# Upper expert weights in halves of four rows a partition, in a mixture-of-experts step bound by its weight stream

## The reference, cut to what matters

```python
def clamped_swiglu(u):
    glu = jnp.minimum(u[..., :D_FF], SWIGLU_LIMIT)
    lin = jnp.clip(u[..., D_FF:], -SWIGLU_LIMIT, SWIGLU_LIMIT)
    return glu * jax.nn.sigmoid(SWIGLU_ALPHA * glu) * (lin + 1.0)
...
    def expert_chunk(args):
        xc, e = args
        return clamped_swiglu(xc @ w_up[e] + b_up[e]) @ w_down[e] + b_down[e]
```

## Time and profile before

| | us |
|---|---|
| median of 3 runs | 1422.34 |
| lowest and highest of them | 1421.0, 1423.39 |
| the profiled execution | 1423.31 |
| its span, first to last instruction | 1421.3 |
| expert stage, from the first upper matmul to the last sum | 482.7 to 1411 |

### The profile page before, as it was taken

One profiled execution on the slowest core, in us unless ns is written; L12 is line 12 of the kernel. 1 busy time (PEld: TensorE's weight loads), 2 busy tenths in 40 slices (PEclk: granted clock), 3 DMA queues, 4 the chain that ended last, 5 costly groups with the idle time before them and its releaser, 6 DMA issues.

```text
span 1421.3 us, 20600 instructions
## 1 busy us (share of the span) xinstructions
PE 1331.1 (94%) x8391; PEld 657.0 (46%) x8392; DVE 494.4 (35%) x1062; ACT 187.1 (13%) x403; POOL 101.7 (7%) x150
## 2 busy tenths in 40 slices
PE   6998879999899999999999999999999999999996
PEld 5887776777688533333333333333333333333332
DVE  2464646444541413223222232313222322233224
ACT  3221112323410200000000000000000000000001
POOL 1001123240000000000000000000000000000000
PEclk9999998999999999999999999999999999999998
DMA  6433339184679899999999999999999999999993
GB/s 187 136 106 83 73 64 289 62 303 130 220 249 358 339 423 430 430 429 431 431 431 431 430 431 431 431 431 430 430 432 431 431 431 431 431 431 431 432 431 145
DMA packets 87027, 479.94 MB, mean 338 GB/s; under 512 B 12740, under 2 KB 52918, under 8 KB 62008
## 3 DMA queue, kind: packets, MB, share of 16 engines
q1 hardware_dynamic: 78664, 452.00, 78.3%
q0 software_dynamic: 7600, 25.45, 5.0%
q10 hardware_dynamic: 704, 1.63, 0.3%
HBM read 478.60 MB, written 8.56 MB: 343 GB/s over the span
## 4 chain that ended last, share of the span: by engine, by line
PE 38%; DMA 26%; DVE 1%; issue 1%; ACT 0%; DVEq 0%; SPq 0%; POOL 0%; POOLq 0%; ACTq 0%
DMA ring<-in_w_up 25%; PE bank L2471 21%; PE bank L2492 9%; PE bank L2442 3%; PE bank L2485 1%; PE bank L2454 1%; PE bank L2424 1%; DVE x L2305 1%; DMA ex_work<-scratch_h,ex_si 1%; PE bank L2430 0%; PE bank L2052 0%; DVE ring L2393 0%; PE bank L238 0%; PE bank L2067 0%; DVE x L2402 0%
## 5 line engine op out<-in xcount | busy, mean ns | idle before, releaser
L2471 PE MATMUL bank<-ring,ex_work 128*64 128x512 f32 x2032 | 457.9, 601 | 18.6 <-DMA ring<-in_w_up 18.5
L2471 PEld LDWEIGHTS bank<-ring,ex_work 128*64 128x64 f32 x2032 | 141.4, 138 | 320.2 <-issue 286.5
L2492 PE MATMUL bank<-ring,ex_work 128*64 128x512 f32 x1024 | 235.2, 613 | 0.0
L2316 DVE TENSOR_SCALAR ex_work<-bank 128x512 f32<-128x512 f32 x32 | 22.1, 691 | 395.1 <-PE bank L2471 395.1
L2305 DVE TENSOR_TENSOR x<-bank,x 128x512 f32<-128x512 f32 (+1 forms) x192 | 117.2, 670 | 100.4 <-PE bank L2442 100.4
L2492 PEld LDWEIGHTS bank<-ring,ex_work 128*64 128x64 f32 x1024 | 72.6, 140 | 160.4 <-issue 160.4
L2442 PE MATMUL bank<-ex_work,ex_back 64*128 64x512 f32 x384 | 91.1, 606 | 1.5 <-ACT ex_work L2236 1.5
L578 PE MATMUL bank<-hT,w_group 128*128 128x264 f32 (+1 forms) x400 | 91.7, 391 | 0.0
L578 PEld LDWEIGHTS bank<-hT,w_group 128*128 128x128 f32 (+1 forms) x400 | 75.4, 189 | 15.2 <-issue 0.7
L2198 POOL DMA_INDIRECT ex_work<-scratch_h,ex_si x31 | 31.7, 1022 | 596.7 <-PE bank L2424 595.9
L2230 ACT ACTIVATE ex_work<-ex_work 128x512 f32<-128x512 f32 x32 | 20.1, 629 | 375.3 <-DVE ex_work L2316 375.3
(11 more groups left out here) (487 smaller groups left out, 1172.3 us busy)
## 6 DMA issues: line engine op xcount, KB each, us to landing
ring<-in_w_up SPq DMA_DIRECT2D x127, 2048.0 KB, 23.0
ring<-in_w_down SPq DMA_DIRECT2D x64, 2048.0 KB, 26.6
w_group<-in_w_in SPq DMA_DIRECT2D x12, 1024.0 KB, 5.3
w_cmp<-in_w_in SPq DMA_DIRECT2D x8, 1024.0 KB, 8.9
ring<-in_w_out SPq DMA_DIRECT2D x8, 512.0 KB, 7.0
out_win_s<-in_state_win_kv POOLq DMA_DIRECT2D x1, 4088.0 KB, 30.8
x<-in_x_prompt SPq DMA_DIRECT2D x4, 512.0 KB, 4.8
win_rows<-in_state_win_kv SPq DMA_DIRECT2D x4, 512.0 KB, 5.3
```

The source lines that it names most:

```text
L2471: mm = mmul(banks[n // 2][lo:lo + SLOTS, :], B["xT"][:, k % 4, SLOTS * (k // 4):SLOTS * (k // 4) + SLOTS], (ninth[:, k, :] if e_ninth and ...
L2492: mm = mmul(banks[4][SLOTS * n:SLOTS * n + SLOTS, :], B["hT"][:, k % 4, SLOTS * (k // 4):SLOTS * (k // 4) + SLOTS], slot_of(8 + 4 * half + ...
```

## The change

The upper matrix is laid out with four neighbouring rows on a partition. From expert 3 on it is moved in two halves of 512 rows (4 MB, runs of 32 KB) instead of four quarters. The first is issued when step 3 of the expert before is done, the second when all steps are; TensorE waits before steps 0 and 4 alone. `half_up` does this. Experts 0 to 2 and the second half of expert 31 move in quarters still: half of the columns of a home, runs of 16 KB at a distance of 32 KB (`upper_quarter`), with waits as before; the first half of expert 0 goes in one transfer. The step of the transposes becomes four, and `gain_columns` is turned to match. The ring has two upper homes of 4 MB and four lower of 2 MB, over the same memory; the transfers in the merge are put in another order, with a quarter of expert 0 ahead of expert 1's lower matrix.

```diff
-        pairs = [at(f"ring{i}", [P, 2, 2 * FF], z) for i, z in enumerate(
-            [DEAD, DEAD + PAIR, DEAD + 2 * PAIR, SEL + 4 * PAIR] + [SEL + PAIR * i for i in range(4)])]
+        upper = [at(f"ring_up{i}", [P, 4, 2 * FF], z) for i, z in enumerate((DEAD, SEL + 3 * PAIR))]
+        lower = [at(f"ring_down{i}", [P, 2, 2 * FF], z) for i, z in enumerate((SEL, SEL + PAIR, SEL + 2 * PAIR, DEAD + 2 * PAIR))]
...
+        def upper_half(e, i):
+            return a["w_up"][0][e, 512 * i:512 * i + 512, :].rearrange("(p c) n -> p c n", c=4)
+
+        def upper_quarter(sp, e, q):
+            cs = slice(2 * (q % 2), 2 * (q % 2) + 2)
+            sp.dma_start(upper[q // 2][:, cs, :], upper_half(e, q // 2)[:, cs, :]).then_inc(ring_in[2 * q], 16)
...
                     sp.wait_ge(outs.sem, 16 * 9)
-                    upper_weights(sp, 0, (0, 1))
+                    sp.dma_start(upper[0][:], upper_half(0, 0)).then_inc(ring_in[0], 16)
                     sp.wait_ge(mix_ok, KD)
                     bias_loads(sp)
-                    for e in range(2):
-                        lower_weights(sp, e)
+                    lower_weights(sp, 0, 0)
+                    lower_weights(sp, 0, 1)
+                    upper_quarter(sp, 0, 2)
+                    lower_weights(sp, 1, 0)
                     sp.wait_ge(od, KD)
-                    upper_weights(sp, 0, (2, 3))
+                    upper_quarter(sp, 0, 3)
+                    lower_weights(sp, 1, 1)
...
+                    def half_up(e, i):
+                        if i:
+                            sp.wait_ge(S["up_done"], e)
+                        else:
+                            sp.wait_ge(S["up_used"], 3 * (e - 1) + 2)
+                        sp.dma_start(upper[i][:], a["w_up"][0][bass.ds(e, 1), 512 * i:512 * i + 512, :].rearrange("e (p c) n -> (e p) c n", c=4)
+                                     ).then_inc(ring_in[4 * i], 16)
...
-                    up(1, True, (1, 2, 3))
-                    up(2, True, first_free=True)
+                    quarters(1, (1, 2, 3))
+                    quarters(2, range(4))
                     down(2, 0, True)
-                    up(3, True)
+                    up(3)
...
+                    half_up(NEXP - 1, 0)
+                    sp.wait_ge(S["up_used"], 3 * (NEXP - 1))
+                    upper_quarter(sp, NEXP - 1, 2)
+                    sp.wait_ge(S["up_done"], NEXP - 1)
+                    upper_quarter(sp, NEXP - 1, 3)
+                    down(NEXP - 1, 1, True)
...
-                            elif k == 0:
-                                pe.wait_ge(ring_in[k], 16 * e)
-                            elif k % 2 == 0:
-                                pe.wait_ge(ring_in[k], 16 * (e + 1))
+                            elif k == 0:
+                                pe.wait_ge(ring_in[0], 16 * e)
+                            elif k == 4:
+                                pe.wait_ge(ring_in[4], 16 * (e + 1))
```

More of the change, by code:

```diff
@@ L158, in build @@
         R["in"] = sem("route_consts_in", True)
-        R["gcol"] = sb(ctx, "gain_columns", [P, 4, 2])
+        R["gcol"] = sb(ctx, "gain_columns", [P, 2, 4])
         x = sb(ctx, "x", [P, 3, D])
@@ L2444, in comb, with up @@
                                 mm.then_inc(S["comb"], 1)
-                    def up(e, wait, back, late=False, first_pair=None, e_ninth=False):
+                    def up(e, wait, back, late=False, landed=None, e_ninth=False):
                         if late:
@@ L2462, in up @@
                                 turn_h(e - 1)
[L2463 to L2464 removed]
+                            if landed is not None and k % 2 == 0:
+                                if landed[k // 2] is not None:
+                                    pe.wait_ge(*landed[k // 2])
                             elif k == 0:
[L2466 to L2468 removed]
+                                pe.wait_ge(ring_in[0], 16 * e)
+                            elif k == 4:
+                                pe.wait_ge(ring_in[4], 16 * (e + 1))
                             for n in range(4):
```

59 lines of the change are left out of this document (28 added, 31 removed).

## The result

The changed kernel takes 1426.3 us (median of 20 runs, 1419.3 to 1430.0), the kernel before 1422.2 (20 runs, 1418.2 to 1426.8). The ratio, which goes by the means of the runs (1425.4 and 1422.5), is 1.0021, with a 95% interval of 1.0012 to 1.0031: some 3.0 us slower. The medians lie 4.1 us apart. A second series gave 1.0019 (1.0003 to 1.0034).

What follows compares the result with a forecast made beforehand. The prediction took the landing of expert 30's last upper quarter, set by the DMA stream, plus TensorE's remaining work as the bound; -2.2 + 3.4 + 1.5 = +2.7 us on the 1422.3 median gave 1425.0 us, range 1421.5 to 1430.

Steps and rivals of the forecast that it cites:

- within or slower: Cases for the whole time against the kernel before, about 0.2% being no change: within 0.46, slower 0.47, faster 0.07.
- term 3: Later issue of upper halves: the queue runs short at experts 3 and 17; +1.5 us, bounds 0 and 3.
- What bounds the end: End of the kernel: landing of expert 30's last upper quarter, set by the DMA stream, plus TensorE's remaining 61.6 us.
- Term 1: Upper-matrix stream: fewer, larger packets save a cost per packet, 0.0092 us a MB over 239 MB; -2.2 us, bounds 0 and 3.1 saved.
- Term 2: Tail at expert 30: four steps instead of two remain after the last upper landing; +3.4 us, bounds 1.7 and 5.1.
- 65 us from there to the end: Sign for the tail: time from expert 30's last wait to the end, 65 us instead of 61.6.
- Edits at nothing: Fewer issues, transposes' step, gather beside larger packets (7.2 us could double, covered), merge order, fewer semaphore waits: no cost.
- R1: Rival, faster: packets cost more and the tail is covered; upper stream over 1.2% faster, -4.2 us, 1418; chance 0.05.
- R2: Rival, slower: reads 32 KB apart are slower, 5.5 us of stream per cent lost; 1433 at 1%; chance 0.12.
- R3: Rival, slower: upper packets stay at 16 KB, so no saving; +4.9 us, 1427; chance 0.11.
- some 7300: Sign for the rate: the number of packets by which the changed kernel's count would fall.
- R4: Rival: saving and later issues cancel and the tail is hidden by TensorE getting ahead; -0.7 us, 1422; chance 0.10.

Runs made afterwards that it cites:

- wait_halves: Kernel before, with only TensorE's wait made coarser: a whole half of an upper matrix before steps 0 and 4; transfers, packets and issues unchanged; ratio 1.0014.
- wait_whole: Kernel before, with TensorE waiting for the whole upper matrix (all four quarters) before step 0, for all experts; ratio 1.0324.
- quarters_apart: Kernel before with the new row layout alone: quarters in 16 KB runs 32 KB apart, transposes at a step of four; ratio 1.0002.

## Why the prediction was right, and where its terms were not

The forecast of 1425.0 us, the range, and "within or slower" hold: 1426.3 us, and a ratio that lies at the bound of 0.2% between the two likeliest cases. Three mechanisms were named and all three act. That the sum comes out so near is partly luck: term 3 was priced at a third of its size, and what makes up for it is in part an effect that the prediction does not have.

- **What bounds the end.** Right. The last link through a transfer ends at 1359.2, where the second half of expert 30 lands, and the rest is TensorE's. (The flat stretch of the earlier trace rows is slices 15 to 38, from 533 to 1386 us, so some 850 us and not 890; nothing hangs on it.)
- **Term 1, predicted -2.2.** Right in mechanism and in size. Its 0.0092 us a MB, from the 421 GB/s beside the 431 of the earlier trace rows, is 4.8 ns a packet; measured are 4.7 from 16 KB to 32 KB and 4.7 from 8 KB to 16 KB. With the 0.01 for fewer transfers after gains 0.084 to 0.090 us an expert, over 28.5 experts 2.4 to 2.6 us. Two windows of a few microseconds gave this number; that another two (417 instead of 421) give 3.1 shows how much of the accuracy is chance. By the last landings the gain looks like 3.3 us, but there the shares' drifting apart in before is counted with it.
- **Term 2, predicted +3.4.** Right: +3.6 in `wait_halves` at the same clock, 32 matmuls behind the last wait. In after's profile it shows as 1.7, since the clock did not fall. The "65 us from there to the end" was met at the clock of before, and missed as it was profiled (63.4).
- **Term 3, predicted +1.5.** The mechanism and both places are right; the term was mis-sized: +3.65 by the last landings (1.34 at expert 3, 2.31 at 16 and 17), +4.4 by the mean of the signals (1.7 and 2.7), past its upper bound of 3 either way. The step that failed is to count from the last landing ahead, with a start-up of 2.5 us behind it. For the last share that step is right: in after the half of expert 17 went out 1.0 us ahead of the last landing (952.7 and 953.7), by the step 1.5 are lost, and the half landed 11.14 us behind the transfer ahead, where two transfers of 4.84 would be 9.68. But the other shares had landed from 949.8 on, so their engines lost more; that shows in the 2.4 us of missing bytes, and at the landings behind (10.49 and 6.11 us behind the one ahead for the second half of expert 17 and its last lower transfer, instead of 9.68 and 4.84). In `wait_whole` even 2.8 us ahead were not enough.
- **A term that is missing.** The sixteen shares lie closer together behind a gap. In before the last share lands 2.9 us behind the mean at T, in after 1.8. That takes 1.1 us off.
- **Edits at nothing.** Right: the distance of 32 KB and the step of the transposes by `quarters_apart` (1.0002). The gather got longer, not doubled: GpSimd waits 278.2 us over 30 for it, 9.3 each instead of 7.2, and TensorE nowhere waits for it.

```profile
POOL ex_si L2217 <- DMA ex_work<-scratch_h,ex_si: 278.2, 30, 11.2
```

- **The rivals.** R1 needed a stream over 1.2% faster in the upper halves: 0.09 us of some 19.5 an expert is 0.5%. The ceiling of 435.2 GB/s that the Trainium skill gives ("DMA: Bandwidth & Descriptors", section "Where 436 GB/s comes from") fits the 432 of after over 200 us; single slices of the profile of after, with 436 and 437, lie a little above it. R2 is excluded by `quarters_apart`. The loss at large row pitches that the Trainium skill gives ("DMA: Bandwidth & Descriptors", section "Latency and other measured facts": 207 GB/s of 214 at 512 KiB) does not show at a pitch of 32 KB here: 1.0002. R3 is excluded by 7424 packets of 32 KB, and 8607 packets fewer on the page, where some 7300 were announced; 1183 of them are packets under 512 B (12740 before, 11557 after). R4 needed a hidden tail, and `wait_halves` shows it in full.

The prediction's own sum would be, with the measured terms and the missing one, -2.5 + 3.6 + 4.4 - 1.1 = +4.4. The profiles have +2.6 with the clock's 1.7 us in after's favour, +4.3 without it. The timed difference is +3.0 by the means (interval +1.7 to +4.4), +4.1 by the medians. Since the clock falls in some executions and not in others, at one place or another, part of the difference between 4.4 and 3.0 stays open.

## What to carry to other kernels

Where a stream of transfers sets the time, a larger transfer has three prices: who reads it waits for all of it, its home is free only when all of it is read, and its issue comes that much later. The first is paid once, behind the last landing, and again wherever the reader's lateness delays an issue into a short queue. The others are paid wherever the queue is short. There one should ask for the time between the issue and the landings of the transfer ahead, and not the last of them alone. Over the upper transfers of the fourteen traces (from 505 us on), one issued 1 to 2 us ahead of that last landing came 1.5 us late (median of 9, against 4.84 us for a quarter and 9.67 for a half), 2 to 3 us ahead 1.0 (12), 3 to 4 us 0.3 (18), and from 4 to 10 us ahead still 0.2 to 0.4. So some 4 us are wanted here, not the start-up of a lone transfer. Going from 16 KB packets to 32 KB in two thirds of the bytes was worth 0.3% of the stream, which one or two short gaps use up.

And a finer measure pays: the last landing of a transfer hides what the other engines lost, and shows as a gain or a loss what is only their spread.

## What the runs showed of the hardware

- A packet of 32 KB took 1213 ns at the median, one of 16 KB 611, one of 8 KB 309. The fixed part is 7 to 9 ns a packet by these medians, and 4.7 ns by the landings, from 8 KB to 16 KB and from 16 KB to 32 KB alike.
- The sixteen shares of a transfer do not land together: in before they lay 6.0 us apart at expert 20 and 7.3 at expert 29. After a short queue they came closer (2.2 and 3.1 in after).
- A queue that never falls empty by issues and last landings still loses rate: 344 GB/s from 3.7 us before the last landing ahead, when the first of its sixteen shares had landed, and 2.4 us of stream in all. After an empty queue the rate was back at 410 GB/s 3 to 5 us after the issue.
- From expert 15 to 20 the coarse wait alone cost the stream 1.7 us, the late issue alone nothing, and both 2.3 (149.51, 147.87, 150.14 against 147.83), though the last landings show the wait as free (59.83 against 59.80 from 15 to 17).
- Where the granted clock falls to 0.80 for one product of 32 matmuls, it costs 1.7 us (8.78 against 7.09). In one execution it falls behind the last landing, in another ahead of it, and with it the tail changes by as much as half of what the change does to it.
